# The last down matrix of the expert loops in five transfers instead of two

## The reference, cut to what matters

```
gate, idx = top_k(softmax(h @ router).T, 32)
xs  = h[idx]                                   # per expert: 32 tokens x 1024
hid = silu(xs @ w1[e]) * (xs @ w3[e])          # w1, w3: 1024 x 1024
ys  = (hid @ w2[e]) * gate                     # w2: 1024 x 1024, the down matrix
out = scatter_add(ys, idx)
```

## Time and profile before

| | us |
|---|---|
| median of 3 runs | 3014.35 |
| lowest and highest | 3014.23, 3017.13 |
| span of the profiled execution, first to last instruction | 3016.0 |
| TensorE busy in it | 2677.4 |
| VectorE busy in it | 1330.7 |
| ScalarE busy in it | 490.4 |

### The profile page before, as it was taken

One profiled execution on the slowest core, in us unless ns is written; L12 is line 12 of the kernel. 1 busy time (PEld: TensorE's weight loads), 2 busy tenths in 40 slices (PEclk: granted clock), 3 DMA queues, 4 the chain that ended last, 5 costly groups with the idle time before them and its releaser, 6 DMA issues. The chain is left out here.

```text
span 3016.0 us, 44924 instructions
## 1 busy us (share of the span) xinstructions
PE 2677.4 (89%) x19748; PEld 1652.4 (55%) x19748; DVE 1330.7 (44%) x2509; ACT 490.4 (16%) x1158; POOL 26.4 (1%) x48
## 2 busy tenths in 40 slices
PE   7989999999999999998999989889979898865665
PEld 3467844446767888735753333345449687432323
DVE  2775488442473876586321111131367763100001
ACT  1023200000213000225221111020051311100000
POOL 0000000000000000000000000000000000000000
PEclk9999999999999999998999999999989999978878
DMA  9530255342352676220159999982110007899998
GB/s 358 195 140 26 87 195 223 139 168 112 112 195 71 251 279 248 75 84 29 59 232 402 427 428 428 427 339 46 44 36 30 2 25 301 366 427 428 427 427 353
DMA packets 67938, 651.34 MB, mean 216 GB/s; under 512 B 14880, under 2 KB 26912, under 8 KB 28064
## 3 DMA queue, kind: packets, MB, share of 16 engines
q1 hardware_dynamic: 67744, 648.47, 53.3%
HBM read 644.12 MB, written 4.33 MB: 215 GB/s over the span
## 5 line engine op out<-in xcount | busy, mean ns | idle before, releaser
L375 PE MATMUL ps<-HT,ring 128*128 128x256 f32 (+1 forms) x3152 | 901.3, 444 | 6.4 <-ACT HT L617 2.3
L375 PEld LDWEIGHTS ps<-HT,ring 128*128 128x128 f32 x3152 | 589.0, 190 | 284.5 <-issue 225.8
L2443 PE MATMUL ps<-ring,arena 128*32 128x256 f32 (+1 forms) x2944 | 372.9, 509 | 106.7 <-DMA ring<-in_moe_w 97.2
L477 DVE SCALAR_TENSOR_TENSOR acc<-ring,sil,acc 128x512 f32<-128x512 f32 x616 | 411.7, 744 | 0.0
L375 PE MATMUL ps<-arena,ring 128*128 128x256 f32 (+3 forms) x1232 | 373.6, 464 | 3.4 <-PEq L718 2.2
L2443 PEld LDWEIGHTS ps<-ring,arena 128*32 128x32 f32 (+1 forms) x2944 | 140.8, 131 | 315.0 <-issue 198.3
L375 PEld LDWEIGHTS ps<-arena,ring 128*128 128x128 f32 (+2 forms) x1232 | 230.1, 188 | 139.3 <-issue 119.3
L1042 DVE SCALAR_TENSOR_TENSOR XT<-ps,modcols,XT 128x256 f32<-128x256 f32 x124 | 55.7, 481 | 266.1 <-PE ps L375 140.4
L2464 PE MATMUL ps<-ring,arena 128*32 128x256 f32 x960 | 83.7, 510 | 58.6 <-DMA ring<-in_moe_w 58.6
L2464 PE MATMUL ps<-ring,conv 128*64 128x512 f32 x496 | 112.3, 596 | 24.0 <-DMA ring<-in_moe_w 23.3
L495 ACT ACTIVATE modrows<-ps 128x128 f32<-128x128 f32 x44 | 12.2, 278 | 574.8 <-PE ps L491 574.8
(11 more groups left out here) (431 smaller groups left out, 2611.4 us busy)
## 6 DMA issues: line engine op xcount, KB each, us to landing
ring<-in_moe_w SPq DMA_DIRECT2D x184, 2048.0 KB, 25.6
ring<-in_w_mod SPq DMA_DIRECT2D x24, 2048.0 KB, 8.1
ring<-in_ada_w SPq DMA_DIRECT2D x24, 2048.0 KB, 8.2
ring<-in_w_up SPq DMA_DIRECT2D x16, 2048.0 KB, 12.1
ring<-in_w_down SPq DMA_DIRECT2D x16, 2048.0 KB, 12.4
ring<-in_w_in SPq DMA_DIRECT2D x10, 2048.0 KB, 10.7
ring<-in_od_w_in SPq DMA_DIRECT2D x6, 2048.0 KB, 25.6
arena<-in_moe_w SPq DMA_DIRECT2D x10, 1024.0 KB, 20.4
```

The costliest lines, as they stand in the source:

```text
L375: last = nc.tensor.matmul(bank_of(job, j), lhsT, rhs, start=n == 0, stop=n == len(terms) - 1)
L477: ins = nc.vector.scalar_tensor_tensor(out=acc, in0=weights[:, k, :], scalar=s, in1=acc, op0=ALU.mult, op1=ALU.add)
L2443: last = nc.tensor.matmul(K.ps[M * j:M * j + M, 2 * (e % 2) + i, 0:FW], xs[:, e // 4 % 2, e % 4, 4 * h + k, :], weights((m, e, h), k, slic ...
```

## The change

The second half of expert 15's `moe_w2` becomes four pieces of the stream of 512 KB each (one block of 128 rows by 1024 columns), each in a ring slot of its own with its own landing wait, multiplied by a quarter of the matmuls. This is done in both layers, so `expert_pieces` is three longer in each, and everything behind the loop of layer 0 stands three places later in the stream. The transfers of the unchanged pieces have the same shape as before.

```diff
     def load(self, sp, i):
         if i < len(self.stream):
             src, kc, w = self.stream[i]
-            sp.dma_start(self.ring[:, i % RING, 0:kc * w], src.rearrange("(p n) -> p n", p=P)).then_inc(
+            sp.dma_start(self.ring[:, i % RING, 0:kc * w], src if len(src.shape) == 2 else src.rearrange("(p n) -> p n", p=P)).then_inc(
                 self.sem(f"slot{i % RING}_landed"), 16)
...
-    return order + [("moe_w2", NE - 1, h) for h in range(2)]
+    return order + [("moe_w2", NE - 1, h) for h in range(5)]
+
+def last_parts(e):
+    return [(0, range(4))] + ([(1, range(4))] if e < NE - 1 else [(1 + k, range(k, k + 1)) for k in range(4)])
 
 def plan_experts(K, l):
     for i, (m, e, h) in enumerate(expert_pieces()):
         if i not in PREFETCHED[l]:
-            K.stream.append((K.dram[m][l, e, h].rearrange("p n -> (p n)"), 4, D))
+            if (m, e) == ("moe_w2", NE - 1) and h:
+                K.stream.append((K.dram[m][l, e, 1][:, (h - 1) * D:h * D], 1, D))
+            else:
+                K.stream.append((K.dram[m][l, e, h], 4, D))
...
-                for h in range(2):
+                for h, ks in last_parts(e):
                     pe.wait_ge(*landed(("moe_w2", e, h)))
-                    for k in range(4):
-                        f, c = divmod(4 * h + k, NC)
+                    for k in ks:
+                        f, c = divmod(4 * (h > 0) + k, NC)
                         for j in range(J):
                             last = nc.tensor.matmul(K.ps[M * j:M * j + M, 5, 0:FW], hidT[:, c, M * f:M * f + M],
-                                                    weights(("moe_w2", e, h), k, slice(j * FW, (j + 1) * FW)), start=h == 0 and k == 0,
-                                                    stop=h == 1 and k == 3)
+                                                    weights(("moe_w2", e, h), k - ks[0], slice(j * FW, (j + 1) * FW)), start=h == 0 and k == 0,
+                                                    stop=h > 0 and k == 3)
                     last.then_inc(*K.inc("pieces_used"))
...
-            eng.wait_ge(*K.at("pieces_used", used["moe_w2", e, 1]))
+            eng.wait_ge(*K.at("pieces_used", used["moe_w2", e, last_parts(e)[-1][0]]))
```

## The result

| | before | after |
|---|---|---|
| median of 5 runs, us | 3017.13 | 3031.02 |
| lowest to highest | 3014.23 to 3025.64 | 3027.3 to 3034.83 |
| span of the profiled execution | 3016.0 | 3030.4 |
| time of that execution | not given | 3032.15 |

The ratio is 1.0044, 95% interval 1.0032 to 1.0056: 13.3 us slower, between 9.7 and 16.9. The five runs of before are the three shown earlier and two later ones, at 3021.33 and 3025.64. The forecast had the sign and the mechanism. Its time, 3024.0 with a range up to 3028.5, was too low.

A forecast was written before the change was run, and what follows sets the result against it. Transfers were taken to set the time in the two expert loops. Late od_w_out +9.8, clock behind it +2.0, layer 0's end -0.2, layer 1's end -2.75, scatter's clock +0.8: +9.65 on 3014.35 gives 3024.0 us, range 3019.0 to 3028.5.

The forecast's parts named there:

- The slots and the standstill: Start of out_projection: pieces move three slots, od_w_out is issued late and TensorE waits for it; +9.8 us (8.8 to 10.3).
- The clock behind it: In out_projection after the idle wait: TensorE runs at 1.2 GHz for a while; +2.0 us, bounds 1.0 and 3.0.
- That it reaches the end: Layer 1's expert loop: what delays its first ring load at 2579.63 delays the last landing at 3004.6 by as much.
- The end of layer 0: End of layer 0's expert loop: TensorE's own work replaces the wait for a landing; gain 0.2 us (0 to 0.3).
- The end of layer 1: End of layer 1's expert loop: one quarter instead of 3.45 us behind the last landing; gain 2.75 us (2.6 to 3.0).
- The scatter's clock: Final scatter after layer 1's loop: TensorE may run it at a low clock; +0.8 us, bounds 0 and +3.7.
- The sum: Whole kernel: all terms together add +9.65 us, own range +6.5 to +12.7.
- The base: Whole kernel: median before taken as 3014.35 us, the profiled span being 1.65 above it; the sum was added to this.
- rival 5: Expert loops of both layers: small transfers pay one by one, +10.8 us twice, 3045 us; chance 0.02.

The follow-up runs named there:

- layer 1 alone: Against the kernel before: only layer 1's last half in quarters, layer 0 as before; 3018.51 us, ratio 0.9995; again 3015.41 us, 0.9992.
- aligned: Against the changed kernel: layer 0's down matrix of expert 15 in eight 512 KB transfers, layer 1's quarters kept; 3017.97 us, ratio 0.9997 to before.
- A: Not a run but a distance in each profile: from out_projection's first group-norm matmul (line 1365) to the first ring load of layer 1's loop; before, 62.5 us.
- layer 0 alone: Against the kernel before: only layer 0's last half in quarters, layer 1's whole; 3031.19 us, ratio 1.0041.
- reverse order: Changed kernel with the three ring pieces of the stage's start issued in reverse, od_w_out's first half last; 3036.93 us, ratio 1.0056 to before.
- dummies in the standstill: Changed kernel with 13 dummy matmuls on TensorE before the wait for od_w_out; 3025.01 us, ratio 1.0023 to before.
- B: Not a run but a distance in each profile: from layer 1's first ring load to the final scatter's first matmul; before, 429.5 us.
- the repeat: The changed kernel timed again without any edit; 3030.80 us, ratio 1.0038 to before.

## Why the prediction was right or wrong

**The slots and the standstill: right.** The SP timeline shows the slots as deduced, and the standstill is 9.04 us of idle time where 9.8 was forecast (it ended 8.9 us after the issue at 2523.21, and not 9.5). Undoing the shift in two ways, layer 1 alone and aligned, brings A back to 62.5, and doubling the wait takes A's excess from 12 to 20 us.

**The clock behind it: right.** 2.0 us were taken, with bounds of 1.0 and 3.0. A's excess over 62.5 less the idle time is 3.0 and 2.5 us in the two profiles of the changed kernel, and 1.9 in those of layer 0 alone and of the reverse order. Standstill and clock together were forecast at 11.8 and measured 12.0, 11.7 and 10.5 in three profiles (A less 62.5).

**That it reaches the end: right.** Layer 0 alone, dummies in the standstill and reverse order have an A longer by 10.5, 9.1 and 20.2 us, and their medians are +12.0, +7.1 and +19.0, where the last two also have the gain of the quarters.

**The end of layer 0: right.** 0.2 forecast, 0.5 in the profile; TensorE and not the landing limits it.

**The end of layer 1: mis-sized.** The step was "Behind the last landing one quarter is left in place of 3.45 us. Gain 2.6 to 3.0 us; I take 2.75." One quarter is left, but two parts of the size were wrong. 3.45 us is the pace at 1.2 GHz, which three of four profiles show; at 2.4 GHz, the fourth, the half takes 1.93. And "the last lands when the half landed before" missed by some 0.6 us: it comes later by that. Measured is a gain of B of 0.3 to 2.8 us, 1.8 on average. The lower bound of the term should have come from the half at 2999.90 (1.93 us) in the same rows: 1.93 - 0.86 = 1.1 us. What a piece is worth at the end of a loop whose clock changes between the levels had to be bounded with both levels on both sides. By time the gain is 1.5 and 2.4 us by two ratios, both with intervals that hold zero.

**The scatter's clock: right as a risk.** +0.8 us forecast; in the seven profiles with quarters it is nothing five times and 1.3 and 1.4 us in the other two, 0.4 on average. The upper end of the sum's range took +2.0 for it, and not the bound of +3.7 that the text gives.

**The sum: right, with one error against another.** From the start of out_projection to the end of the span it is 508.5 and 507.9 us in the two profiles of the changed kernel, and 498.9, 497.0 and 498.3 in the three with whole halves in both layers and no dummies. That is +10.1 between the means, less 0.5 for layer 0's end +9.6, where +9.65 was forecast. That it is so near is luck: the gain at the end was taken too large, and so was the clock in the scatter, and the single terms differ by 1 us and more from profile to profile.

**The base: this is the step that put the time out of the range.** "That span is 1.65 above the median, so the median becomes 3014.35 + 9.65 = 3024.0." In the later profiles the run's time is 1.75 us longer than the span (3032.15 against 3030.4), so the profiled execution of before was one of about 3017.8. Laid on that, the sum is 3027.4, and the range of 3019.0 to 3028.5 becomes 3022.4 to 3031.9, which holds the measured 3031.02. The runs of before had their median at 3017.13, 3019.22, 3017.94 and 3017.35 later, 2.8 to 4.9 us above the three first ones, and single runs from 3006 to 3028. Three runs, two of them 0.12 us apart, looked like a firm base and were not; the range allowed 1.5 us for it.

**What remains.** Of the 7.0 us between 3024.0 and 3031.02 the base is 2.8 (3017.13 for 3014.35). The other 4.2 are the effect as timed: by the medians it is +13.9 us, and +11.6 for the repeat, where +9.65 was forecast and +9.6 is found in the profiles behind out_projection. The interval of the repeat (+6.9 to +16) holds that, that of the result (+9.7 to +16.9) has it at its edge. No profile shows another place that differs with the change, and the kernel with whole halves in the changed code shows none by time. The clock in unchanged code makes differences of this size between single runs; that it made this one is likely and not shown. Of rival 5, small transfers that pay one by one, little is seen: 1.25 us from quarter to quarter and 0.6 us at the last landing. The Trainium skill, page "SBUF — State Buffer", section "The DMA setup-cost knee", gives every transfer a fixed cost of about 2 us; in this full queue it isn't paid one by one.

No version here beats the kernel before measurably. Quarters in layer 1 alone is the one to keep, if any: its two ratios are 0.9995 and 0.9992.

## What to carry to other kernels

In a ring whose slot is the piece's number modulo the ring's length, a piece more in one stage moves every later piece to another slot. Where some slots are loaded at another time than others, look up which transfer gets the late place before splitting anything, and keep the number of added pieces a multiple of the ring's length, or put them behind the last such place. A split at the end of a stream is worth at most what is multiplied behind the last landing, read at the full clock as well as at the low one. And a forecast of a time needs a base as well as a sum: three runs of a kernel whose runs spread over 19 us don't give one to 1.5 us, and the time of the profiled execution is one more run to set beside them.

## What the runs showed of the hardware

The whole-run time of one kernel spreads over 19 us on one chip (3006.44 to 3025.58 in 29 runs of before; 18 us on another). The mean granted clock goes with it: 0.961 or 0.962 in the four fastest of these runs, 0.955 to 0.957 in the four slowest. Two profiles of the changed kernel were 7.2 us apart at the start of out_projection with the same instructions behind them, and their windows differ by 7.2 us of granted clock. Where TensorE's idle time was 18.26 us, A grew by 1.9 us beyond it (82.7 - 62.5 - 18.26), no more than the 3.0 and 2.5 behind 9.04 and 9.17. In a full queue, transfers of 512 KB landed 1.25 us apart.
